# A two-layer trunk on one core: where TensorE's small products stand between the big ones of a weight tile

## What is computed

```
for i in range(2):
    h = rms_norm(x, norm_mix[i])
    x = x + (gmlp(h) if i == 0 else s5(h))           # token mixer
    h = rms_norm(x, norm_ffn[i])
    x = x + (silu(h @ w1[i]) * (h @ w3[i])) @ w2[i]  # SwiGLU, 2048 -> 5632 -> 2048
    gate = sigmoid(rms_norm(x, norm_ple[i]) @ ple_w_gate[i])
    x = x + gate * (p[i] @ ple_w_proj[i])
return rms_norm(x, norm_final)
# gmlp: u, v = split(gelu(h @ w_in)); v = layer_norm(v)
#       sv[t] = sum over s <= t in a chunk of 128 of w_s[head, t, s] * v[s] + b_s   (16 heads of 128)
#       (u * sv) @ w_out
# s5:   u = h @ w_in, 128 groups of 16 channels with 64 complex states each;
#       s[t] = lam_bar * s[t-1] + b_bar u[t];  y = Re(C s) + d * u
#       val, gate = split(gelu(y) @ w_out);  val * sigmoid(gate)
```

## Time and profile before

| | |
|---|---|
| timed runs, median | 2367.42 us |
| the profiled execution | 2365.84 us, span 2364.1 us |
| TensorE (PE) busy | 2301.6 us, 97%, 11853 matmuls |
| VectorE (DVE) busy | 1336.5 us, 57% |
| ScalarE (ACT) busy | 1034.3 us, 44% |
| GpSimd (POOL) busy | 474.8 us, 20% |
| granted TensorE clock, mean | 0.99 of full |
| memory traffic | 206 GB/s mean |

### The profile page before, as it was taken

One profiled execution on the slowest core, in us unless ns is written; L12 is line 12 of the kernel. 1 busy time (PEld: TensorE's weight loads), 2 busy tenths in 40 slices (PEclk: granted clock), 3 DMA queues, 4 the chain that ended last, 5 costly groups with the idle time before them and its releaser, 6 DMA issues.

```text
span 2364.1 us, 29152 instructions
## 1 busy us (share of the span) xinstructions
PE 2301.6 (97%) x11853; PEld 1904.2 (81%) x11853; DVE 1336.5 (57%) x1402; ACT 1034.3 (44%) x1252; POOL 474.8 (20%) x438
## 2 busy tenths in 40 slices
PE   5989999999999999999998999999999999999997
PEld 4868888888888888888887788888888888888886
DVE  4786655554555555555656665545445445445565
ACT  3534444444444444444543344444443344444443
POOL 1067304554666355300000000000000000000001
PEclk8999999999999999999999999999999999999999
DMA  6545667766667667666877966566655566665553
GB/s 215 174 152 177 189 194 228 230 216 215 224 219 240 213 217 223 207 214 212 272 245 252 303 212 187 189 192 193 188 187 193 192 193 190 189 190 188 187 205 134
DMA packets 276551, 487.03 MB, mean 206 GB/s; under 512 B 52049, under 2 KB 56545, under 8 KB 276033
## 3 DMA queue, kind: packets, MB, share of 16 engines
q1 hardware_dynamic: 256752, 477.42, 62.6%
q10 hardware_dynamic: 18896, 4.26, 0.8%
q0 software_dynamic: 768, 3.48, 0.4%
HBM read 453.65 MB, written 31.46 MB: 205 GB/s over the span
## 4 chain that ended last, share of the span: by engine, by line
PE 95%; DVE 3%; issue 1%; DMA 1%; ACT 0%; ACTq 0%; SPq 0%; DVEq 0%
PE PS L1385 30%; PE PS L1387 30%; PE PS L1386 30%; PE PS L1414 2%; DVE WLO L976 1%; PE PS L1494 1%; DVE V L1194 1%; PE PS L1632 0%; PE PS L1624 0%; PE PS L1504 0%; PE PS L1606 0%; DMA TE<-tabe 0%; PE PS L1469 0%; DVE OP L995 0%; DVE STAT L1007 0%
## 5 line engine op out<-in xcount | busy, mean ns | idle before, releaser
L976 DVE TENSOR_TENSOR WLO<-RAW,WHI 128x1024 fp32r<-128x1024 f32 x792 | 1038.0, 1314 | 933.0 <-ACT WHI L717 930.9
L1385 PE MATMUL PS<-WHI,OP 128*128 128x512 f32 x3136 | 1235.1, 394 | 27.3 <-DVE WLO L976 27.3
L717 ACT ACTIVATE WHI<-RAW 128x1024 fp32r<-128x1024 f32 x792 | 839.3, 1062 | 941.2 <-PE PS L1387 926.3
L1387 PE MATMUL PS<-WHI,OP 128*128 128x512 f32 x3136 | 1224.0, 390 | 0.0
L1386 PE MATMUL PS<-WLO,OP 128*128 128x512 f32 x3136 | 1223.3, 390 | 0.0
L1385 PEld LDWEIGHTS PS<-WHI,OP 128*128 128x128 f32 x3136 | 590.5, 188 | 154.1 <-issue 33.8
L1387 PEld LDWEIGHTS PS<-WHI,OP 128*128 128x128 f32 x3136 | 590.3, 188 | 124.0
L1386 PEld LDWEIGHTS PS<-WLO,OP 128*128 128x128 f32 x3136 | 591.0, 188 | 119.5
L701 POOL TENSOR_TENSOR ON<-X,GF 128x1024 f32<-128x1024 f32 x3 | 9.9, 3308 | 994.5 <-DVE X L1255 994.5
L640 POOL TENSOR_TENSOR TA<-BRAW,FAC 128x64 f32<-128x64 f32 x16 | 7.1, 445 | 367.3 <-DMA BRAW<-in_s_b_im 367.3
L749 ACT ACTIVATE S<-PS,RC 128x512 f32<-128x512 f32 x68 | 43.1, 685 | 61.9 <-PE PS L1387 61.8
(11 more groups left out here) (184 smaller groups left out, 998.3 us busy)
## 6 DMA issues: line engine op xcount, KB each, us to landing
RAW<-in_ffn_w SPq DMA_DIRECT2D x528, 512.0 KB, 4.2
RAW<-in_gm_w_in SPq DMA_DIRECT2D x64, 512.0 KB, 4.3
RAW<-in_ple_w_gate SPq DMA_DIRECT2D x64, 512.0 KB, 4.3
RAW<-in_s_w_out SPq DMA_DIRECT2D x64, 512.0 KB, 4.5
RAW<-in_gm_w_out SPq DMA_DIRECT2D x32, 512.0 KB, 4.1
RAW<-in_s_w_in SPq DMA_DIRECT2D x32, 512.0 KB, 4.8
tabq<-QS SPq DMA_DIRECT2D x16, 512.0 KB, 5.3
tabd<-DT SPq DMA_DIRECT2D x16, 512.0 KB, 6.0
```

Source lines behind the costliest of these rows:

```text
L717: A_.activation(WHI[:, t % RING, :], RAW[:, t % RING, :], ACT.Copy).then_inc(hi_ready, 1)
L976: V_.tensor_tensor(WLO[:, t % RING, :], RAW[:, t % RING, :], WHI[:, t % RING, :].bitcast(F32), ALU.subtract).then_inc(lo_ready, 1)
L1385: T_.matmul(dst[:, th, :], hi, WHI[:, slot, f], start=begin, stop=False)
L1387: last = T_.matmul(dst[:, th, :], lo, WHI[:, slot, f], start=False, stop=finish)
```

## The change

Each lump is taken apart. The functions of the small products get an index i, and between(t, i) is called behind each of the twelve big matmuls of tile t; it puts out the i-th piece of the lump that stood behind tile t - 1. A piece is one transpose (turn, turn_u, turn_tables, turn_ws, turn_p, set_up) or one product (mix), two products for turn_c, one product and then four times two for taps, four products for into_states (8 pieces) and for out_of_states (12 pieces: four, then eight). The waits stand ahead of piece 0, so behind the first big matmul of the next tile; the semaphore increments stay on the same instructions. split_used's increment stays on the twelfth big matmul. The four lumps of x stay as they are. The loops over columns are otherwise the same, and the order of the instructions of each lump is kept.

```diff
 def tile(t, dst, block_, first, last_one):
...
+                        i = 6 * kk + 3 * th
                         T_.matmul(dst[:, th, :], hi, WHI[:, slot, f], start=begin, stop=False)
+                        between(t, i)
                         T_.matmul(dst[:, th, :], hi, WLO[:, slot, f], start=False, stop=False)
+                        between(t, i + 1)
                         last = T_.matmul(dst[:, th, :], lo, WHI[:, slot, f], start=False, stop=finish)
-                last.then_inc(split_used, 1)
+                        if kk == TK - 1 and th == 1:
+                            last.then_inc(split_used, 1)
+                        between(t, i + 2)
 
...
+            def turn(q, i):
...
+                m, th = i // 2, i % 2
+                src = Z[:, th, P * m:P * m + P] if row is None else X[:, th, NW * c + P * m:NW * c + P * m + P]
+                at = TOK * (m % 2) + P * th
+                last = T_.transpose(PS[:, bank + m // 2, at:at + P], src, IDENT[:, :])
+                if i % 4 == 3:
+                    last.then_inc(turned, 1)
...
+            def turn_c(r, i):
+                if i == 0:
+                    if r == 0:
+                        pe.wait_ge(c_in, 32)
+                        pe.wait_ge(z_ready, Z_COUNT["us", NT - 1])
+                    else:
+                        pe.wait_ge(ct_ready, r)
+                ri, m = i // 4, i % 4
+                for g in range(2):
+                    at = 4 * QP * CH * ri + QP * CH * m
+                    last = T_.matmul(PS[ST * g:ST * g + ST, 6, at:at + QP * CH], CN[:, ri, 4 * r + m, :],
+                                     IDENT[:, :].rearrange("p (q g c) -> p q g c", g=2, c=CH)[:, :, g, :],
+                                     start=True, stop=True)
+                if i == 7:
+                    last.then_inc(ct_done, 1)
...
+            def taps(b, i):
+                if i == 0:
+                    pe.wait_ge(d_ready, b + 1)
+                    pe.wait_ge(qs_ready, b + 1)
+                    T_.matmul(PS[:, 6, 0:P], IDENT[:, :], DG[:, :, :].rearrange("p c j -> p (c j)"), start=True, stop=False)
...
+                    k = i - 1
                     for ri in range(2):
                         last = T_.matmul(PS[32 * k:32 * k + 32, 6, 0:P], BB[:, ri, k, :],
                                          DT[:, k, ri, :, :].rearrange("p c j -> p (c j)"), start=False, stop=(ri == 1))
...
+                bl, q = s // QP, s % QP
+                for ri in range(2):
+                    for g in range(2):
+                        at = DP * NC * ri + NC * (QP * bl + q)
+                        last = T_.matmul(PS[ST * g:ST * g + ST, 4 + i, at:at + NC], TQ[i][:, bl, q, ri, ST * g:ST * g + ST],
+                                         UP[n % 2][:, 2 * i + bl, 2 * q + g, :], start=True, stop=True)
+                if s == 7:
+                    last.then_inc(in_done, 1)
...
+                if s < 4:
+                    bl, g = s // 2, s % 2
+                    f = slice(P * bl, P * bl + P)
+                    for q in range(QP):
+                        T_.matmul(PS[NC * q:NC * q + NC, bank + g, f], UP[n % 2][:, 2 * i + bl, 2 * q + g, :],
+                                  TKK[tab][:, bl, 2 * q + g, :], start=(bl == 0), stop=False, skip_group_check=True)
+                else:
+                    bl, ri, half_q = (s - 4) // 4, (s - 4) // 2 % 2, s % 2
+                    f = slice(P * bl, P * bl + P)
+                    for q in (2 * half_q, 2 * half_q + 1):
+                        for g in range(2):
+                            half = slice(ST * g, ST * g + ST)
+                            last = T_.matmul(PS[NC * q:NC * q + NC, bank + g, f], SD[i][half, ri, QP * bl + q, :],
+                                             TD[tab][half, bl, q, ri, :], start=False, stop=(ri == 1), skip_group_check=True)
+                    if s == 11:
+                        last.then_inc(out_of, 1)
+
...
+            def between(t, i):
+
+                if t - 1 in AFTER and i < 8:
+                    turn(AFTER[t - 1], i)
+                if t - 1 == SET_AT and i < 8:
+                    if i < 4:
+                        set_up(i)
+                    else:
+                        turn_p(0, i - 4)
+                if t - 1 == PT1_AT and i < 4:
+                    turn_p(1, i)
+                for w in range(2):
+                    if t - 1 == WT_AT[w] and i < 8:
+                        turn_ws(w, i)
+                for n in range(NT):
+                    if t - 1 == MIX_AT[n] and i < 8:
+                        mix(n, i)
+                    if t - 1 == CT_AT[n] and i < 8:
+                        turn_c(n, i)
+                    if t - 1 == UT_AT[n] and i < 8:
+                        turn_u(n, i)
+                for b in range(KB):
+                    if t - 1 == BUILD_A[b] and i < 8:
+                        turn_tables(b, i)
+                    if t - 1 == BUILD_B[b] and i < 5:
+                        taps(b, i)
+                for d in range(DUOS):
+                    if t - 1 == INTO_AT[d] and i < 8:
+                        into_states(d, i)
+                    if t - 1 == OUT_AT[d]:
+                        out_of_states(d, i)
...
-                    hooks(t)
...
+                    if stage == "v" and n == 0 and j in (0, 1, 3):
+                        for i in range(8):
+                            turn({0: 1, 1: 2, 3: 3}[j], i)
```

More of the change, by code:

```diff
@@ L66 @@
 DEPTH_OF = {name: depth for name, _, depth in STAGES}
+COLS_OF = {name: cols for name, cols, _ in STAGES}
 def start(stage, n=0):
@@ L1390, in OP_of @@
+                        between(t, i + 2)
             def OP_of(k):
                 return PT[:, k - 100, :] if k >= 100 else OP[:, k, :]
[L1393 to L1407, removed]
-                    else:
[L1409 to L1416, removed]
@@ L1429, in free @@
                     pe.wait_ge(x_ready, X_COUNT[s, m])
[L1431 to L1435, removed]
-                    T_.transpose(PS[:, 6, PAIRS * i:PAIRS * i + PAIRS], AN[:, i, :], IDENT[0:PAIRS, 0:PAIRS])
[L1437 to L1447, removed]
@@ L1449, in turn_ws @@
-            def turn_ws(i):
-                if i == 0:
-                    pe.wait_ge(ws_masked, 1)
-                    pe.wait_ge(pt_ready, 1)
-                    pe.wait_ge(p_ready, 1)
-                else:
[L1455 to L1502, removed]
+            def set_up(i):
+                if i == 0:
+                    pe.wait_ge(operand_ready, 8)
+                    pe.wait_ge(s5_in, 64)
+                    pe.wait_ge(ldt_spread, 1)
+                if i < 3:
+                    T_.transpose(PS[:, 6, PAIRS * i:PAIRS * i + PAIRS], AN[:, i, :], IDENT[0:PAIRS, 0:PAIRS])
+                else:
+                    T_.transpose(PS[:, 6, 3 * PAIRS:3 * PAIRS + HEADS], BS[:, :], IDENT[0:HEADS, 0:HEADS]).then_inc(set_done, 1)
@@ new lines, in turn_p, with turn_ws @@
+            def turn_p(layer, i):
+                if i == 0:
+                    pe.wait_ge(p1_in if layer else p_in, 16)
+                    if layer:
+                        pe.wait_ge(act_took, ACT_COUNT["out1", 2])
+                f, th = i // 2, i % 2
+                at = TOK * f + P * th
+                last = T_.transpose(PS[:, 7, at:at + P], PN[:, th, P * f:P * f + P], IDENT[:, :])
+                if i == 3:
+                    last.then_inc(p_turned, 1)
+            def turn_ws(w, h):
+                if h == 0:
+                    if w == 0:
+                        pe.wait_ge(ws_masked, 1)
+                        pe.wait_ge(pt_ready, 1)
+                        pe.wait_ge(p_ready, 1)
+                    else:
+                        pe.wait_ge(wt_ready, w)
+                last = T_.transpose(PS[:, 6 + h // 4, P * (h % 4):P * (h % 4) + P], WN[:, 8 * w + h, :], IDENT[:, :])
+                if h == 7:
+                    last.then_inc(wt_done, 1)
@@ new lines, in mix @@
+            def mix(n, i):
+                if i == 0:
+                    pe.wait_ge(v_ready, n + 1)
+                    if n == 0:
+                        pe.wait_ge(wt_ready, 2)
+                    else:
+                        pe.wait_ge(z_ready, Z_COUNT["us", n - 1])
+                th, m = i // QB, i % QB
+                h = QB * n + m
+                last = T_.matmul(PS[:, 6 + th, P * m:P * m + P], WT[:, h, :], V[:, th, P * h:P * h + P], start=True, stop=True)
+                if i == 7:
+                    last.then_inc(mixed, 1)
@@ new lines, in turn_tables @@
+            def turn_tables(b, i):
+                if i == 0:
+                    pe.wait_ge(q_ready, b + 1)
+                    if b:
+                        pe.wait_ge(exp_ready, b)
+                    else:
+                        pe.wait_ge(ct_ready, 4)
+                last = T_.transpose(PS[:, 6 + i // 4, P * (i % 4):P * (i % 4) + P],
+                                    QT[:, i // 2, i % 2, :, :].rearrange("p c j -> p (c j)"), IDENT[:, :])
```

(53 more changed lines are left out.)

86 lines of the change are left out of this document (37 added, 49 removed).

## The result

The changed kernel takes 2487.91 us (median of four runs, 2485.50 to 2491.26), the kernel before 2367.09 beside it: ratio 1.0515, 95% interval 1.0502 to 1.0528. That is 121 us slower. The forecast was 2443 and 2400 to 2470: right in its direction, and 45 us short. The profiled execution took 2485.50 us over a span of 2483.8.

A forecast was written before the change was run, and what follows sets the result against it. TensorE's own stream was taken as the bound, carrying 95% of the chain of waits. Terms summed to +82 us, taken as +78, less 2 for waits: +76 on 2365.84, 2441.8, so 2443 us timed; range 2400 to 2470.

The forecast's parts named there:

- full-array products: 69 lumps of eight, placed singly: 0.96 us against 0.88 per eight, +5.5 us; mix about +0.4 us.
- taps: 16 lumps of 1.03 us become one full-array group and four narrow groups of 0.47 us, 2.11 us: +17.3 us.
- turn_c: 4 lumps of 1.28 us become 8 groups of 0.44 us each, 3.52 us: +9.0 us.
- into_states: 8 lumps of 2.19 us become 8 groups of 0.55 us each, 4.4 us: +17.7 us.
- out_of_states: 8 lumps of 2.30 us become 4 groups of 0.57 and 8 of 0.49 us, 6.2 us: +31.2 us.
- set_up: Four small 64- and 16-row transposes, spread: about +1 us.
- correction of the steps: Steps inside groups, taken at the lump's mean, include longer ones between groups: sum lowered from +82 to +78 us.
- waits that move: Late results stay covered; in the state-space stage the stall shrinks from 3.8 to 3.3 us: some -2 us over three.
- clock: Rival: all 16 tiles with spread into_states or out_of_states run at 1.2 GHz, +43 us more, 2486 us; chance 0.09.
- The forecast's own sign for this step: For taps: a tile holding its spread pieces would be 2.1 us longer than 2.72.
- out_of_states' second kind of piece: The 8 later groups of each out_of_states: 0.09 + 7 x 0.014 + 0.30 = 0.49 us each.
- The stall itself: TensorE's wait ahead of out_of_states for VectorE's chain in the state-space stage: 3.3 us instead of 3.8.

The follow-up runs named there:

- experiment 2: Changed kernel with all narrow-form products and set_up back in lumps, full-array transposes and mix still spread: 2373.84 us, ratio 1.0029 to the kernel before.
- experiment 4: Changed kernel, taps still in five pieces, each narrow one holding two products for two different column strips instead of the same strip: 2474.12 us, ratio 1.0453.
- experiment 5: Changed kernel with taps in three pieces: the full-array product, then two narrow pieces of all four column strips: 2457.63 us, ratio 1.0385.
- experiment 6: Changed kernel with VectorE's copies to UC ahead of the odd duo's scan instead of behind it, for n = 1 to 3: 2457.36 us, ratio 1.0385.
- experiment 8: Changed kernel with out_of_states alone back in lumps: 2436.86 us, ratio 1.0301 to the kernel before.
- Experiment 1: Changed kernel with taps alone back in one lump between two tiles: 2454.99 us, ratio 1.0367 to the kernel before.
- experiment 7: Kernel before the change, with VectorE's copies to UC ahead of the odd duo's scan: 2375.32 us, ratio 1.0036.

## Why the prediction was wrong

By its own steps, from the profile after (cost after less cost before, times the count):

| step | forecast | measured |
|---|---|---|
| full-array products | 5.5 + 0.4 | (0.94 - 0.885) x 69 = 3.8, mix 0.1 |
| taps | 17.3 | (0.23 + 4 x 0.76 - 1.03) x 16 = 36 |
| turn_c | 9.0 | (3.75 - 1.28) x 4 = 9.9 |
| into_states | 17.7 | (4.5 - 2.19) x 8 = 18.5 |
| out_of_states | 31.2 | (5.99 + 0.66 - 2.30) x 8 = 34.8 |
| set_up | 1 | 1.0 |
| correction of the steps | -4 | (none) |
| waits that move | -2 | about 0 |
| clock (cost at the half level, after less before) | 0 (rival: +43) | 20.2 - 4.4 = 16 |
| sum | 76 | 120 (the timed runs: 121) |

**Right:** that TensorE's stream is all that counts; that a single transpose pays its weight load anyway; that every visit to a narrow form is paid, in by 0.09 and out by 0.26 to 0.32 us, in each piece; that late results are covered, but for some 2 us (experiment 2). The mechanism that was forecast is the larger part of the result.

**The first failure is the term of taps:** "0.09 + 3 steps 0.06 + 0.32 = 0.47 each". Its steps came from "the lump's mean", 0.39 us over 15 steps, as if these were instructions one behind the other. They were four chains side by side, one per column strip, and the mean step is the real one divided by four. (Three of the mean steps are 0.08 and not 0.06, a small slip beside it.) A piece with one strip has three whole steps, 0.33 to 0.35 us instead of 0.06; 64 pieces make 17 to 19 us. Experiments 4 and 5 show it, with the number of passages held and then halved. The forecast's own sign for this step, a taps tile 2.1 us longer than 2.72, came out at 3.2. The forecast had even corrected the sum by -4 us in the other direction. The same slip, smaller, is in out_of_states' second kind of piece, 0.56 us each instead of 0.49 where the first kind was right (0.55 against 0.57): +3.6 us in the whole of out_of_states. That a piece of the second kind fills only half of the tiles that ran side by side in the lump is the likely reason; no run tests it for this product.

The page "TensorE: Matmul & The Clock Gate" of the Trainium skill, Part 3, says that weight loads overlap running matmuls only where the row group differs. Here the four strips of taps use all 128 rows and differ in their columns alone. In the piece of experiment 5 the eight weight loads lie within 0.16 us, beside the first matmuls, which start with them at 432.37:

```profile
432.37 0.16 PEld L1520 LDWEIGHTS PS<-DT,BB 128*32 128x32 f32 x8 [0.24 <-issue]
```

A window that ends 0.05 us behind 432.37 holds four matmuls, started within 0.32 - 0.30 = 0.02 us, so the starts of the four strips lie 0.007 us apart (0.013 in the lump of the kernel before). The measurement decides: this overlap needed no other row group.

**The second is the clock**, a rival with 0.09. It was priced for all 16 sparse tiles; it came at three of the eight out_of_states and cost 16 us more than before. The forecast held that "the narrow lumps alone don't bring it down", which is so; it missed that a wait which already was there brings the fall, and that the change decides how long it stays (experiments 6 and 8). The earlier trace rows showed the fall. The stall itself was forecast rightly, 3.3 us against 3.4. The 20.2 us are experiment 6's 30.5 less 10.3 for the waits. What the half level had been worth in the kernel before, 4.4 us, is from the three tiles concerned: their length (10.19, 9.57, 10.37 us) less tile, lump and wait.

Experiment 1 gave 33 us where the trace gives 36, and the runs of one kernel lie within 4 to 6 us, so sums of single steps are good to some 3 us.

## What to carry to other kernels

Order small products by their form of the array, not by their fit into gaps: each visit to a narrow form, in and out again, cost 0.35 to 0.41 us here, so narrow products belong together, and neighbours should lie in different column strips. When a step time is read from a lump, ask how many chains run in it before it is used for a piece. A short stall is cheaper before dense work than before sparse work: behind waits of 3 to 4 us TensorE's clock was at the 1.2 GHz level for 3 to 7 us in the one case and for 14 to 20 in the other.

## What was not expected of the hardware

Column strips over the same rows run side by side, with starts 0.007 us (experiments 4 and 5) to 0.013 us apart (the lump before), while instructions in one strip follow at 0.11 to 0.13. Sparse tiles (twelve big matmuls in 8.7 us) kept the full clock for as long as nothing stood still ahead of them: granted 1.00 through the stage in experiment 6, 0.68 in the tiles behind the 3.4 us wait. Taking away a wait of TensorE made the kernel slower (experiment 7), as UP's load then landed late.
